# First feed-forward stage of a two-layer encoder: four opening units on scaled rows, root and shift applied to their results

## What is computed

```python
cond = silu(c)
mod = cond @ ada_w[l] + ada_b[l]          # nine groups of 1024: shift, scale, gate for each sub-layer
y = x * rsqrt(mean(x * x) + 1e-6) * ffn1_norm_g[l]
h = y * (1 + sc1) + sh1
gate, up = split(h @ w_in)                # w_in: 1024 x 5632
x = x + 0.5 * g1 * ((silu(gate) * up) @ w_out)
```

## Time and profile before

| what | us |
|---|---|
| median of three runs | 2325.67 |
| lowest and highest run | 2321.43 and 4048.39 |
| profiled execution, its own time | 2327.99 |
| its span, first to last instruction | 2326.3 |
| PE busy | 2302.5 (99%) |
| DVE busy | 1284.4 (55%) |
| ACT busy | 852.4 (37%) |
| POOL busy | 113.7 (5%) |
| mean granted clock of TensorE | 0.995 |

### The profile page before, as it was taken

How to read it: one execution, slowest core, us unless ns; L and a number is a source line. 1 busy time by engine, 2 the same in 40 slices (tenths; PEclk the granted TensorE clock), 3 DMA queues, 4 the chain that set the end, 5 groups by cost and what they waited for, 6 DMA issues and landing times.

```text
span 2326.3 us, 37275 instructions
## 1 busy us (share of the span) xinstructions
PE 2302.5 (99%) x14356; PEld 1872.5 (80%) x14356; DVE 1284.4 (55%) x1860; ACT 852.4 (37%) x1277; POOL 113.7 (5%) x220
## 2 busy tenths in 40 slices
PE   8999999999999999999999999999999999999998
PEld 6888888777778888888878888887777788888887
DVE  4554556786457664433475545577756576443334
ACT  5231224542455543223342212345225555331222
POOL 1000000020000000000000000101000000000000
PEclk8999999999999999999999999999999999999999
DMA  8564563353334344433245645623332353453231
GB/s 317 193 211 154 178 204 125 100 145 96 99 114 151 112 136 153 145 99 104 95 135 189 209 138 196 212 96 106 116 102 91 118 178 95 148 170 101 90 113 60
DMA packets 96182, 325.38 MB, mean 140 GB/s; under 512 B 12904, under 2 KB 15624, under 8 KB 95040
## 3 DMA queue, kind: packets, MB, share of 16 engines
q1 hardware_dynamic: 57936, 215.56, 28.5%
q0 software_dynamic: 23760, 82.48, 11.3%
q10 hardware_dynamic: 14368, 25.70, 3.1%
HBM read 306.34 MB, written 14.73 MB: 138 GB/s over the span
## 4 chain that ended last, share of the span: by engine, by line
PE 93%; DVE 3%; ACT 1%; issue 1%; DMA 1%; SPq 0%; DVEq 0%; POOL 0%; ACTq 0%; POOLq 0%
PE PS L566 81%; PE PS L1187 4%; PE PS L895 1%; DVE h L1898 1%; PE PS L581 0%; PE PS L1135 0%; PE PS L1161 0%; PE PS L604 0%; DVE wl L1652 0%; DVE t_buf L1925 0%; DMA ada<-in_ada_first_dram 0%; PE PS L1170 0%; PE PS L886 0%; ACT wh L1264 0%; DMA ada_raw<-in_ada_w_dram 0%
## 5 line engine op out<-in xcount | busy, mean ns | idle before, releaser
L1652 DVE TENSOR_TENSOR wl<-raw,wh 128x1024 fp32r<-128x1024 f32 (+2 forms) x360 | 466.1, 1295 | 775.0 <-ACT wh L1264 774.3
L566 PE MATMUL PS<-uh,wh 128*128 128x512 f32 x2176 | 860.8, 396 | 3.5 <-DVE wl L1652 2.1
L566 PE MATMUL PS<-ul,wh 128*128 128x512 f32 x2176 | 847.9, 390 | 0.0
L566 PE MATMUL PS<-uh,wl 128*128 128x512 f32 x2176 | 847.9, 390 | 0.0
L1264 ACT ACTIVATE wh<-raw 128x1024 fp32r<-128x1024 f32 (+2 forms) x360 | 402.3, 1118 | 869.2 <-PE PS L566 851.4
L566 PEld LDWEIGHTS PS<-uh,wh 128*128 128x128 f32 x2176 | 408.3, 188 | 99.9 <-issue 7.4
L566 PEld LDWEIGHTS PS<-uh,wl 128*128 128x128 f32 x2176 | 408.5, 188 | 86.5
L566 PEld LDWEIGHTS PS<-ul,wh 128*128 128x128 f32 x2176 | 408.8, 188 | 80.7
L566 PE MATMUL PS<-hh,wh 128*128 128x512 f32 x726 | 283.1, 390 | 0.0
L566 PE MATMUL PS<-hl,wh 128*128 128x512 f32 x726 | 282.5, 389 | 0.0
L566 PE MATMUL PS<-hh,wl 128*128 128x512 f32 x726 | 282.5, 389 | 0.0
(11 more groups left out here) (302 smaller groups left out, 1663.5 us busy)
## 6 DMA issues: line engine op xcount, KB each, us to landing
raw<-in_ffn_in_dram SPq DMA_DIRECT2D x176, 512.0 KB, 3.6
ada_raw<-in_ada_w_dram POOLq DMA_DIRECT2D x144, 512.0 KB, 3.9
raw<-in_mix_in_dram SPq DMA_DIRECT2D x88, 512.0 KB, 3.6
raw<-in_ffn_out_dram SPq DMA_DIRECT2D x32, 768.0 KB, 4.3
raw<-in_ffn_out_dram SPq DMA_DIRECT2D x32, 640.0 KB, 3.9
g_in<-gates_dram ACTq DMA_DIRECT2D x48, 256.0 KB, 3.1
ada<-in_ada_first_dram SPq DMA_DIRECT2D x8, 1024.0 KB, 16.5
raw<-in_mix_up_dram SPq DMA_DIRECT2D x16, 512.0 KB, 3.6
```

The source lines that it names most:

```text
L566: mm = e.matmul(PS[:, bank, :], w[:, j % 2, k * P:(k + 1) * P], v[:, k, :], start=(k == 0 and w is wh and v is xh), stop=(k == K - 1 and w ...
L1652: TTo(wl[:, j % 2, 0:K * P], raw[:, j, 0:K * P], wh[:, j % 2, 0:K * P], ALU.subtract)\
```

## The change

It concerns the start, up to unit 8 of the first sub-layer.

- The loads have a new order: one pair of x rows, then lot 0, constants, two raw units, and so on. Each lot of `ada_first` holds two rows of one kind now: lots 0 to 3 the scales, lots 4 to 7 the shifts. `cond` comes last. POOL loads the first two `ada_raw` buffers ahead of its tables.
- `opening_units` takes the place of `first_pair`: units 0 to 3 multiply rows that are only scaled, which need no root. The rows of units 0 and 1 stand between the sums of lots 0 to 3, those of unit 2 between the sums of lots 4 to 7. Shift sums of all four units (128 records) come before unit 2's last row. Wakes of 16, 14 and 7 matmuls stand before, and between, the first sums.
- VectorE multiplies the root to the results of four units and adds the shift; ScalarE and VectorE overwrite `uh` and `ul` with the rows scaled by the root and shifted, each when unit 3 has used it. Unit 4 is the first to multiply these.
- One modulation product is done early (behind the first two results). The three others of the first body stand, with the two of the next use, at the use of unit 5, ahead of unit 8's split.

```diff
-LAG = 3
-WAKE = 32
+WAKE = (16, 14, 7)
...
+                            tokens(0)
+                            ada_lot(0)
+                            for t, src in ((ident_q, "ident_q"), (eps, "eps"), (ada_b, "ada_b")):
+                                e.dma_start(t[:, :], a[src]).then_inc(consts_in.sem, 16)
+                            e.dma_start(norm_g[:, :, :], a["norm_g"]).then_inc(consts_in.sem, 16)
+                            for j in range(2):
                                 load(0, 0, j, a[name + "_in"][j], KD)
+                            tokens(1)
+                            ada_lot(1)
+                            for t, src in ((ident, "ident"), (final_g, "final_g")):
+                                e.dma_start(t[:, :], a[src]).then_inc(late_in.sem, 16)
+                            for j in range(2, 4):
+                                tokens(j)
+                                ada_lot(j)
+                            for j in range(2, 4):
+                                load(0, 0, j, a[name + "_in"][j], KD)
+                            for lot in range(4, ADA_LOTS):
+                                ada_lot(lot)
+                            e.dma_start(cond[:, :], a["c"].broadcast_to([P, KD * P])).then_inc(cond_in.sem, 16)
                         elif half == 0:
...
-                        norms = 0 if half or start else norm_index(l, first // SUB) + 1
+                        norms = 0 if half else stage_index(l, first // SUB) + 1
...
+            e.wait_ge(ada0_in[ADA_LOTS - 1].sem, 16)
+            for j in range(2):
+                e.dma_start(ada_raw[:, j, :], a["ada_w"][ADA_FIRST + j]).then_inc(ada_in[j].sem, 16)
+
...
-                with e.Fori(0, ADA_MAIN // 2) as i:
+                with e.Fori(0 if l else 1, ADA_MAIN // 2) as i:
...
+            def shift_sums(units):
+
+                for j in range(0, units, 2):
+                    for k in range(KD):
+                        for h in range(4):
+                            c0 = k * P + HALF * h
+                            mm = e.matmul(PS[32 * h:32 * h + 32, 7, j * HALF:(j + 2) * HALF]
+                                          .rearrange("p (a n) -> p a n", a=2),
+                                          mod[:, k:k + 1].broadcast_to([P, 32]), raw[:, j:j + 2, c0:c0 + HALF],
+                                          start=(k == 0), stop=(k == KD - 1), skip_group_check=True)
+                mm.then_inc(shift_mm.sem, 1)
+
...
+                def rows(j, ks):
+                    unit(0, j, j, KD, banks[j], uh, ul, row_there if j < 2 else None, ks, j == 3)
+                first_sums(0)
+                wake(WAKE[1])
+                rows(0, range(0, 2))
+                rows(1, range(0, 2))
+                first_sums(1)
+                wake(WAKE[2])
+                first_sums(2)
+                rows(0, range(2, 4))
+                rows(1, range(2, 4))
+                rows(0, range(4, 6))
+                first_sums(3)
+                rows(1, range(4, 6))
+                e.wait_ge(ssq_done.sem, ssq_done.at(0, 6))
+                token_sums(ssq[:, :], True, False)
+                e.wait_ge(sq_done.sem, sq_done.at(0, 8))
+                mm = token_sums(sq[:, 1, :], False, True)
+                mm.then_inc(norm_mm.sem, 1)
+                rows(0, range(6, 8))
+                rows(1, range(6, 8))
+                e.wait_ge(consts_in.sem, 16 * 4)
+                e.wait_ge(late_in.sem, 16 * 2)
+                e.wait_ge(rstd_done.sem, rstd_done.at(0, 1))
+                spread()
+                first_sums(4)
+                rows(2, range(0, 2))
+                first_sums(5)
+                rows(2, range(2, 4))
+                first_sums(6)
+                rows(2, range(4, 6))
+                first_sums(7)
+                rows(2, range(6, 7))
+                e.wait_ge(first_mods.sem, ADA_LOTS // 2)
+                shift_sums(4)
+                rows(2, range(7, 8))
+                rows(3, range(0, 8))
+
...
+                    opens = (l, s, half) == (0, 0, 0)
+                    if opens:
+
+                        e.wait_ge(silu_done.sem, silu_done.at(0, 1))
+                        unit(0, RAW, 0, KD, 0, uh, ul, shifted_there)
+                        for j in range(1, 4):
+                            in_unit(1, j)
+                    with e.Fori(1 - half + opens, F // 2) as i:
...
+            peeled = 2 if opened else 1 if deferred is not None or bodies == 2 else 0
+            if opened:
+                body(1, False)
...
+            def scaled_row(k):
+
+                e.wait_ge(first_scale.sem, k // 2 + 1)
+                e.activation(uh[:, k, :], x[:, k, :], ACT.Identity, scale=scale_eff[:, k:k + 1], bias=eps[:, 2:3])\
+                    .then_inc(yh_done.sem, 1)
+
+            def shifted_row(k):
+
+                if k < KD - 1:
+                    e.wait_ge(row_used.sem, k + 1)
+                else:
+                    multiplied(0, 3)
+                e.wait_ge(t_done.sem, k + 1)
+                e.wait_ge(first_mods.sem, k // 2 + 1)
+                e.activation(uh[:, k, :], xn[k][:, :], ACT.Identity, bias=mod[:, k:k + 1]).then_inc(uh_done.sem, 1)
+
...
+            squares(range(0, 2))
+            split(0, 0, 0, 0, KD)
+            e.wait_ge(consts_in.sem, 16 * 4)
+            scaled_row(0)
+            scaled_row(1)
+            split(0, 0, 0, 1, KD)
+            squares(range(2, 4))
+            scaled_row(2)
+            scaled_row(3)
+            squares(range(4, 8))
+            for k in range(4, KD):
+                scaled_row(k)
             e.activation(warm[:, 0:1], eps[:, 0:1], ACT.Sqrt)
             root(0, 0)
-
-            def first_row(k):
...
+            split(0, 0, 0, 2, KD)
+            e.wait_ge(rstd_mm.sem, 1)
+            e.activation(gate_hold[:, :], PS[:, 6, :], ACT.Copy).then_inc(first_root.sem, 1)
+            split(0, 0, 0, 3, KD)
             e.sem_inc(mods_done.sem, 1)
+            e.wait_ge(cond_in.sem, 16)
+            e.activation(cond[:, :], cond[:, :], ACT.Silu).then_inc(cond_done.sem, 1)
+            shifted_row(0)
+            first_silu(0)
+            shifted_row(1)
+            split(0, 1, 0, 0, KD)
+            for k in range(2, 6):
+                shifted_row(k)
+            first_hh(0)
+            shifted_row(6)
+            shifted_row(7)
+            split(0, 1, 0, 1, KD)
+            first_silu(1)
+            first_hh(1)
             for l in range(DEPTH):
...
+                            if opened and isinstance(i, int) and (i, j) == (1, 1):
+                                ada_main(0, 0, 1)
+                                for b in range(2):
+                                    ada_main(0, 1, b)
...
+            def first_lo(k):
+
+                e.wait_ge(yh_done.sem, k + 1)
+                e.wait_ge(first_scale.sem, k // 2 + 1)
+                STT(out=ul[:, k, :], in0=x[:, k, :], scalar=scale_eff[:, k:k + 1], in1=uh[:, k, :], op0=ALU.mult,
+                    op1=ALU.subtract).then_inc(yl_done.sem, 1)
 
             def normed(k):
...
+                e.wait_ge(first_root.sem, 1)
+                STT(out=xn[k][:, :], in0=x[:, k, :], scalar=scale_eff[:, k:k + 1], in1=gate_hold[:, :], op0=ALU.mult,
+                    op1=ALU.mult).then_inc(t_done.sem, 1)
...
+            split(0, 0, 0, 2, KD)
+            first_sums(4)
+            normed(0)
+            normed(1)
+            first_sums(5)
+            normed(2)
+            normed(3)
+            split(0, 0, 0, 3, KD)
+            first_sums(6)
+            first_sums(7)
+            first_times_root(0, 0, silu_s[:, 0, :])
+            first_times_root(1, 2, h32[:, 0, :])
+            e.wait_ge(cond_done.sem, 2)
+            ada_main(0, 0, 0)
+            normed(4)
+            normed(5)
+            shift_columns(0, 0)
+            normed(6)
+            shifted_lo(0)
+            normed(7)
+            shifted_lo(1)
+            split(0, 1, 0, 0, KD)
+            first_h(0)
             for k in range(2, KD):
-                first_sums(k)
-                if k + 1 < KD:
-                    normed(k + 1)
-                first_lo(k)
-            e.wait_ge(cond_done.sem, 2)
+                shifted_lo(k)
+            split(0, 1, 0, 1, KD)
+            first_times_root(2, 1, silu_s[:, 1, :])
+            first_times_root(3, 3, h32[:, 1, :])
+            e.wait_ge(late_in.sem, 16 * 2)
+            first_hl(0)
+            first_h(1)
+            first_hl(1)
             for l in range(DEPTH):
```

233 lines of the change are left out of this document (110 added, 123 removed).

## The result

The changed kernel takes 2331.98 us (median of nine runs, 2330.64 to 2334.77), the kernel before 2325.67 us (nine runs, of which one took 4048.39 us and is left out of the ratio). The ratio is 1.0031, 95% interval 1.0021 to 1.0042: slower by 0.3%, within 2%. Forecast were 2328.0 us and 2319 to 2335. The profiled execution of after took 2330.64 us, span 2327.9.

The account below looks back on a forecast made before the run. The prediction took TensorE's matmuls as the bound (81% of the span). Its terms, -7.85 + 8.0 + 2.2 = +2.35 us, on the median of 2325.67 gave 2328 us, range 2319 to 2335.

Parts of the forecast that it names:

- "issue": TensorE's opening: waits the profile calls issue, placed nowhere; 1.0 us taken, bounds 0 and 4.3 (-1.0 and +3.3).
- a rival (2333 us): Opening, 13 to 24 us: the granted clock falls there too, +5 us, time 2333, chance 0.18.
- What bounds, and the opening's times: TensorE is the bound; a landing line and prices put sums 0 from 9.3 to 10.4, unit 1's end at 32.1 us.
- Four units done at 50.0: Opening: from unit 1's end TensorE hardly waits; 17.9 us of work ends unit 3 at 50.0, before 1.0 is added.
- Unit 4 directly behind: After unit 3: unit 4, the first on shifted rows, runs 50.3 to 55.8 us, before 1.0 is added.
- The lead of 7.85: End of unit 5: 62.65 us in the changed kernel against 70.50 before, so 7.85 us ahead.
- The five products: Ahead of unit 8's split: from first start a, refill waits let unit 8 start at a+14.2; TensorE idle 8.0 us.
- The clock behind the gap: Behind TensorE's idle time at unit 8: the granted clock is low, 2.2 us lost.
- Sum: Whole change: -7.85 + 8.0 + 2.2 = +2.35 us.
- Covered products: Rival, five products ahead of unit 8: no refill is waited for, no clock lost; 2319 us, chance 0.12.
- Slow refills: Rival, five products ahead of unit 8: refills take 8.3 us each, idle 16.7 us; 2337 us, chance 0.05.
- "The opening wins nothing": Rival, opening: rows still come one at a time, so +10 us; 2336 us, chance 0.05.

Follow-up runs that it names:

- wake_less: Changed kernel without the third group of wake matmuls (7 calls, 14 records); 2329.26 us, ratio 1.0019 to the kernel before.
- warm_gap: Changed kernel with 30 matmuls of ones into an unused bank behind unit 7, filling TensorE's idle time; 2329.98 us, ratio 1.0021.
- wake_first: Changed kernel without the second and third groups of wake matmuls (14 and 7 calls), only the first kept; 2331.65 us, ratio 1.0033.
- held_refill: Changed kernel, four products early, no third wake group, two refills held until unit 4's weights landed, two products between units 6 and 7's splits; 2319.82 us.

## Why the prediction was right

The time was inside the range, 4 us above the forecast, and the mechanism was the one forecast: a row of products paced by its refills, a gap of idle TensorE, a low clock behind it. The opening's lead was not: it came to less than half of the forecast, 4.64 us less, where the bound given for "issue" was 3.3. The time stayed in the range since the other terms were nearly right and since the range was wide enough to hold most of a rival (2333 us) that did not come; that is luck in part. Step by step:

- **What bounds, and the opening's times.** Sums 0 at 9.26 (forecast start 9.3), first row 13.75 (behind the wakes at 13.4), sums 2 at 20.47 (forecast 19.4, behind a lot that landed later than the line had it). Unit 1 ended at 33.1, not 32.1.
- **Four units done at 50.0, plus 1.0 of "issue".** This is the step that failed in size. They were done at 54.35 (the last start, 54.12, and 0.23), 3.35 late. 1.0 came with unit 1; "issue" was 1.77 (1.33 + 0.44), not 1.0; the spread took 0.99, not 0.3; some 0.9 is in ten switches between sums and rows, where the next start comes 0.1 us later than within a group. "Issue" itself is within its bound of 4.3, but every term fell on the same side. The prediction could place "issue" nowhere; by the table above before's two waits, 1.30 and 2.13 us, and after's two stand behind loads of instructions.
- **Unit 4 directly behind.** It began at 55.91, not 51.3: another 1.26. Its weights' refill is issued behind the shift sums, so a stall there costs twice. wake_less shows the two together: without the stalls unit 4 began at 53.23, and the median fell by 2.7.
- **The lead of 7.85.** It was 3.21 (4.64 less: 1.0 + 2.35 + 1.26, and 0.03 in units 4 and 5, which took 11.38 where 11.35 were forecast).
- **The five products.** Forecast a+5.85, a+11.7 and unit 8 at a+14.2; the trace has a+5.83, a+11.52 and a+13.95. That the fourth would find its buffer full was wrong (it waited 0.79), without effect, since the fifth waits for the third. Idle 7.61, forecast 8.0.
- **The clock behind the gap.** 2.15 in the trace, 2.0 by warm_gap, forecast 2.2. One of its two supports was misread: a clock of 0.59 over 4 us is 3.3 us at half speed and 1.6 lost, not 3.9 and 1.9.
- **Sum.** +2.35 forecast, +6.55 by the same terms as measured.
- **The rivals.** The clock did not fall in the opening: 1.00 from 8 to 80. It would have without the fillers of the second group, but by wake_first against wake_less it would have cost 0.8 to 2.4 us, so the +5 of that rival was too high as well. Covered products: no, VectorE waited 6.7 us for them (3.45 + 0.79 + 2.43). Slow refills: no, 3.8 to 4.8 us. "The opening wins nothing": it won 3.2 with the stalls and is what makes held_refill faster than before.

## What to carry to other kernels

Jobs that share a few buffers are paced by the refills: five put off and done in a row on two buffers wait for two refills, and whatever stands behind them on that engine waits too, however short each job is. Do them while the bound engine waits for something else. Moved whole to another place, such a row takes its wait along. Removing two waits may give less than their sum, when the work moved early starts transfers beside the one that the path waits for; holding such transfers back until that one has landed can give the gain back (here together with two products put elsewhere). A wait that the profile calls "issue" can be a load of instructions: set its end beside the packets of the instruction queue.
